# A ring of four slots for gathered table rows, and a residual that stays in SBUF

## What is computed

```python
def _peer(hn, w_query, sub_keys, expert_down, expert_up):
    q = (hn @ w_query).reshape(b, s, PEER_HEADS, 2, PEER_QUERY_DIM // 2)
    sc = jnp.einsum('bshcd,hckd->bshck', q, sub_keys)
    v1, i1 = lax.top_k(sc[..., 0, :], PEER_TOPK)
    v2, i2 = lax.top_k(sc[..., 1, :], PEER_TOPK)
    ...
    top, pos = lax.top_k(cand, PEER_TOPK)      # 8 heads x 16 experts per token
    gate = jax.nn.softmax(top, axis=-1)
    ...
        u = expert_down[ib]                    # rows of a table of 16384 x 1024
        act = jax.nn.gelu(jnp.einsum('bld,blhkd->blhk', hb, u), approximate=False)
        coef = (gb * act)
        vv = expert_up[ib]
        return jnp.einsum('blhk,blhkd->bld', coef, vv)
    ...
h = h + _peer(hn, ...)
```

## Time and profile before

| | us |
|---|---|
| median of 3 runs | 4510.15 (4506.05 to 4513.31) |
| the profiled execution | 4505.03 |
| its span, first to last instruction | 4503.1 |
| expert stage in it | from 3314.7, its first load, to the end |
| busy: TensorE, VectorE, ACT, POOL | 4046.4, 3025.7, 2273.3, 1124.3 |
| moved by DMA | 1082.32 MB, mean 240 GB/s |

### The profile page before, as it was taken

How to read it: one execution, slowest core, us unless ns; L and a number is a source line. 1 busy time by engine, 2 the same in 40 slices (tenths; PEclk the granted TensorE clock), 3 DMA queues, 4 the chain that set the end, 5 groups by cost and what they waited for, 6 DMA issues and landing times. The chain is left out here.

```text
span 4503.1 us, 60284 instructions
## 1 busy us (share of the span) xinstructions
PE 4046.4 (90%) x22760; PEld 3234.1 (72%) x22760; DVE 3025.7 (67%) x3742; ACT 2273.3 (50%) x2916; POOL 1124.3 (25%) x547
## 2 busy tenths in 40 slices
PE   6897669999999999999699779789879999999999
PEld 6786646656555655655479777678779999988887
DVE  5254468888888888888446352254489877688884
ACT  3332146667677677676325235332225998533332
POOL 2121100000000000000132222132224555666662
PEclk9898879999999999999799889899889999999999
DMA  2222079999999999999423422232236899999995
GB/s 87 66 67 78 20 269 349 359 364 368 364 368 361 360 360 367 363 369 361 149 95 94 143 73 69 84 112 71 89 117 230 302 349 348 360 361 367 368 343 191
DMA packets 506172, 1082.32 MB, mean 240 GB/s; under 512 B 23570, under 2 KB 209170, under 8 KB 494712
## 3 DMA queue, kind: packets, MB, share of 16 engines
q1 hardware_dynamic: 465416, 936.49, 58.2%
q0 software_dynamic: 40560, 143.16, 8.6%
HBM read 1001.57 MB, written 77.97 MB: 240 GB/s over the span
## 5 line engine op out<-in xcount | busy, mean ns | idle before, releaser
L1605 DVE TENSOR_TENSOR ffn_low<-ffn_raw,ffn_high 128x2048 fp32r<-128x2048 f32 (+1 forms) x576 | 1189.5, 2109 | 257.4 <-ACT ffn_high L1558 257.4
L1558 ACT CAST ffn_high<-ffn_raw 128x2048 fp32r<-128x2048 f32 (+1 forms) x576 | 987.0, 1765 | 409.2 <-DMA ffn_raw<-in_w_down 126.5
L2850 ACT CAST peer_high<-peer_raw 128x1024 fp32r<-128x1024 f32 x256 | 256.2, 1050 | 446.2 <-PE peer_ps L2832 268.1
L1452 POOL DMA_INDIRECT scratch_h<-ffn_result,ffn_y_rows x16 | 46.3, 2896 | 1344.0 <-DVE ffn_result L1597 1344.0
L296 PE MATMUL peer_ps<-peerbuf_hnT_high,peer_high 128*128 128x384 f32 x1024 | 353.2, 345 | 27.3 <-DVE peer_low L2656 23.6
L298 PE MATMUL peer_ps<-peerbuf_hnT_low,peer_high 128*128 128x384 f32 x1024 | 344.3, 336 | 0.0
L297 PE MATMUL peer_ps<-peerbuf_hnT_high,peer_low 128*128 128x384 f32 x1024 | 344.3, 336 | 0.0
L2656 DVE TENSOR_TENSOR peer_low<-peer_raw,peer_high 128x1024 fp32r<-128x1024 f32 x192 | 260.4, 1383 | 104.4 <-ACT peer_high L2850 100.8
L296 PE MATMUL ffn_gate_p<-ffn_high,ffn_x_high 128*66 128x512 f32 (+1 forms) x768 | 290.1, 378 | 21.1 <-DVE ffn_low L1605 21.1
L296 PE MATMUL ffn_up_p<-ffn_high,ffn_x_high 128*66 128x512 f32 (+1 forms) x768 | 288.2, 375 | 3.1 <-DVE ffn_low L1605 3.1
L296 PE MATMUL ffn_down_p<-ffn_high,ffn_t_high 128*66 128x512 f32 x704 | 279.9, 398 | 11.8 <-DVE ffn_low L1605 11.8
(11 more groups left out here) (522 smaller groups left out, 10004.3 us busy)
## 6 DMA issues: line engine op xcount, KB each, us to landing
ffn_raw<-in_w_gate SPq DMA_DIRECT2D x80, 2048.0 KB, 9.6
ffn_raw<-in_w_up SPq DMA_DIRECT2D x80, 2048.0 KB, 9.9
ffn_raw<-in_w_down SPq DMA_DIRECT2D x80, 2048.0 KB, 10.5
peer_raw<-in_peer_down_t SPq DMA_DIRECT2D x64, 1024.0 KB
peer_raw<-in_peer_up_t SPq DMA_DIRECT2D x64, 1024.0 KB
scratch_a<-peer_gelu SPq DMA_DIRECT2D x64, 384.0 KB
scratch_g<-peer_spread SPq DMA_DIRECT2D x24, 1024.0 KB
peer_spread<-scratch_g SPq DMA_DIRECT2D x16, 1536.0 KB, 11.9
```

The costliest lines, as they stand in the source:

```text
L1452: pool.indirect_dma_start(h_dram, bass.IndirectOffsetOnAxis(ap=y_rows[:, 0:1], axis=0), result[:, :], None, compute_op=ALU.add).then_inc(y ...
L1558: act.copy(half_of(high, q, h), half_of(raw, q, h)).then_inc(high_done, 1)
L1605: dve.tensor_tensor(half_of(low, q, h), half_of(raw, q, h), half_of(high, q, h).bitcast(F32), ALU.subtract).then_inc(low_done, 1)
L2850: act.copy(high[:, q % 2, cols], raw[:, q % PR_RAW, cols]).then_inc(high_done, 1)
```

## The change

The ring has four slots: the three tiles of `hn` and `h[:, NT, :]`. The three residual tiles of `h` stay where they are; their store, their load, both semaphores and the scratch tensor are gone. Nothing else is edited.

```diff
-ROW_RING = 7
+ROW_RING = 4
...
-        rows = [hn[:, i, :] for i in range(DENSE)] + [h[:, NT, :]] + [h[:, i, :] for i in range(DENSE)]
+        rows = [hn[:, i, :] for i in range(DENSE)] + [h[:, NT, :]]
         assert len(rows) == ROW_RING
...
                 load_down(1)
-                sp.dma_start(h_dram.rearrange("t p d -> p t d"), h[:, 0:DENSE, :]).then_inc(h_out, 16)
                 for q in range(PEER_BLOCKS + 6):
...
                 sp.wait_ge(row_used, n_rows)
-                sp.dma_start(h[:, 0:DENSE, :], h_dram.rearrange("t p d -> p t d")).then_inc(h_back, 16)
                 sp.dma_start(out[DENSE * P:NT * P, :], h[:, DENSE, :]).then_inc(stored, 16)
...
                     if n >= ROW_RING:
                         pool.wait_ge(row_used, n - ROW_RING + 1)
-                    elif n == DENSE + 1:
-                        pool.wait_ge(h_out, 16)
...
-                dve.wait_ge(h_back, 16)
                 for t in range(DENSE):
                     dve.wait_ge(tile_summed, t + 1)
```

More of the change, by code:

```diff
@@ L2579, in finish, with peer_experts @@
         dve.sem_inc(self.finished, 1)
-def peer_experts(nc, io, hn, hnT, h, ident, found, a_dram, g_dram, h_dram, out):
+def peer_experts(nc, io, hn, hnT, h, ident, found, a_dram, g_dram, out):
     plan, at = peer_plan()
@@ L2636, in peer_experts @@
             st.sem(x) for x in ("product_done", "c_high_done", "c_low_done", "tile_summed", "added", "stored"))
-        idx_done, row_used, dots_gelu, coef_done, h_out, h_back, gated, minus_done, distance, group_taken_dve = (
-            st.sem(x) for x in ("idx_done", "row_used", "dots_gelu", "coef_done", "h_out", "h_back", "gated", "minus_done",
+        idx_done, row_used, dots_gelu, coef_done, gated, minus_done, distance, group_taken_dve = (
+            st.sem(x) for x in ("idx_done", "row_used", "dots_gelu", "coef_done", "gated", "minus_done",
                                 "distance", "group_taken_dve"))
@@ L3073, in second_block @@
     g_dram = nc.dram_tensor("scratch_g", [G_LOADS, P, G_BATCHES, G_KEYS * G_BATCH], F32).ap()
-    hd_dram = nc.dram_tensor("scratch_hd", [DENSE, P, D], F32).ap()
     acum_dram = nc.dram_tensor("scratch_acum", [SSD_HEADS, SEQ], F32).ap()
@@ L3346, in second_block @@
             query_scores(nc, io, x, hn, hnT, ident, *found)
-            peer_experts(nc, io, hn, hnT, x, ident, found, a_dram, g_dram, hd_dram, out)
+            peer_experts(nc, io, hn, hnT, x, ident, found, a_dram, g_dram, out)
 def two_blocks(nc, io, out):
```

## The result

The changed kernel takes 4715.5 us (median of four runs, 4697.6 to 4719.8), the kernel before 4511.6 beside it: a ratio of 1.0447, 95% interval 1.0433 to 1.0461. It is slower, as forecast, but by 204 us where 102.5 were forecast, and outside the range. The profiled execution took 4713.3 us, with a span of 4711.5.

The account below looks back on a forecast made before the run. TensorE was taken as the bound. Residual -1, blocks without groups +6.5, entry +12 and second half +85 summed to +102.5 us on the profiled 4505.03, forecast 4607 us, range 4535 to 4680.

Parts of the forecast that it names:

- First half, blocks with group work: Blocks at 3520 to 3878: later dots delay the next low, but some 3 us of slack remain, so 0.
- Clock: 0: New TensorE pauses bring lower clock, but slower columns eat pause, not time: 0, upper bound 27 us.
- The second half: Expert stage's second 64 blocks: 5.2 us more per three blocks over 16.3 loops, +85 us.
- the right loop: Second half: c_low, a load, product, same-block gather, accumulate, lows, c_low; 12.9 + A + G = 30.3 us per three blocks.
- A: Second half: SP's load of an a tile, taken as 7.2 us for three, 12 for the fourth: 8.4 us.
- G: Second half: POOL's same-block gather of 512 KB, taken as 9.0 us, next to the waited rows.
- The five blocks without groups: First half, blocks without group work: 9.6 us each where they take 8.3 now, +6.5 us, bounds 0 and 15.
- the entry: Entry to the second half: late first product and the same-block gather behind it delay TensorE, +12 us, bounds 4 and 22.
- The residual's gain of 1 us: Store and reload gone: gain of 1 us for a quieter queue at the stage's start, bounds 0 and 3.
- worse: Rival: TensorE joins the second half's loop through ACT's split and lower clock counts; about 4740 us, chance 0.05.
- a DMA share near 0.8: Sign of the forecast case: the second half's DMA share falls to about 0.8.
- if it grows, the slack of 3 us was wrong: Sign: the first half's stretch with group work should keep its length; growth would refute its 3 us of slack.

Follow-up runs that it names:

- experiment 2: Changed kernel with a third PSUM bank for the group results: 4627.8 us, ratio 1.0255 to the kernel before.
- experiment 4: Changed kernel with each gather issued in the block in which its slot's row is used, not the block after: 4539.7 us, ratio 1.0059.
- experiment 15: Changed kernel, two PSUM banks; gathers issued as slots free in blocks 20 to 62, ahead of the product from 63; a load before weight load: 4503.2 us, ratio 0.9979.
- experiment 8: Changed kernel with filler TensorE work (third group computed three more times) ahead of its wait in the first half: 4678.4 us, ratio 1.0369.
- experiment 9: Changed kernel with 16 filler matmuls ahead of the c_low wait in every third block from 70 to 112: 4715.9 us, ratio 1.0443.
- experiment 1: Kernel before with a ring of four, its store and reload of the residual kept: 4693.6 us, ratio 1.0402.
- experiment 3: Changed kernel with POOL's gathers of a block issued ahead of its product, not behind it: 4626.9 us, ratio 1.0237.
- experiment 11: Changed kernel with SP issuing the a tile's load ahead of the block's weight and g loads: 4675.1 us, ratio 1.0358.
- experiment 10: Changed kernel with gathers of half a row, 256 KB for 512, in the second half alone: 4670.0 us, ratio 1.0352.
- experiment 12: Changed kernel with a third PSUM bank, POOL's gathers ahead of its product and SP's a load ahead of its weight load: 4515.1 us, ratio 1.0014.

## Why the prediction was right and wrong

**The failed step** is "First half, blocks with group work": "Some 3 us of slack, so 0." It took as deadline the next use of low, ACT's split at 3720.40. The deadline that comes first is another: behind the waiting dots stands, right behind the low, VectorE's copy of a group out of PSUM, and TensorE waits for it inside the same block (50.5 us over 15 in the trace after). The prediction listed what is queued behind the wait, "the weight split (low) and c_low of the next block", and left the copy out, though VectorE's order in a block has it between them and the dots. In the trace of before that copy never held anything, and no row of a wait named it. It measured +94.1 us: experiment 2 removed the wait and 90 us of it, experiments 4 and 15 the late gathers and as much.

**Its second error** is in the same step: POOL's issue times were carried over from before (3703.96, 3705.22), as if POOL ran free. POOL's gathers stand behind its half of the split, which waits for ACT's, and that waited 124.4 us for TensorE in 16 of these blocks, so a late third group delays the next gathers. That made a loop, and not a one-time shift.

**Clock: 0** failed for the first half, where TensorE is a link of the loop: 43 us (experiment 8). The Trainium skill (TensorE: Matmul & The Clock Gate, section Terms) puts the penalty of throttled time at about that time multiplied by 1 - K/N, where K of every N clock pulses pass; at 4/8 that is a half. By that rule the 95.6 us would cost 47.8, an estimate, and the 43 of experiment 8 agree. For the second half the reason given, "TensorE is not a link of the loop", does not hold as it stands: the chain passes through TensorE in five places, with 11.6 us more than at full clock. That is well under the 37 us, an estimate, that the same rule gives for the 75 us, so by the chain most of the time at the lower clock ate pause there, as the prediction said. Experiment 9 can't show it, since its added work may cancel the gain.

**The second half** came out as forecast, 91.4 us for 85, by the right loop but with two wrong sizes that cancel. These are the links of the changed kernel, the mean of the 16 turns from block 65 to 113, measured between the starts and ends of the instructions:

| link, us | taken | measured |
|---|---|---|
| c_low's end to the a load's issue | 0.1 | 0.15 |
| the a load, issue to its product's start | 8.4 | 10.1 |
| product and gap | 2.25 | 2.1 |
| gather, issue to its accumulate | 9.0 | 7.2 |
| accumulate, two lows, c_low | 4.65 | 5.0 |
| to the c_low of the next block | 5.9 | 6.6 |
| sum | 30.3 | 31.1 |

(Over all of blocks 64 to 115 it is 516.8 / 17 = 30.4.) A was 1.7 us too short. A term is missing from it: in these turns of experiments 1 and 8 the product started 1.4 and 1.8 us after the load had landed, because POOL was still issuing the gathers of the block before. G was 1.8 us too long. It had been read from the few gathers of the kernel before that VectorE waited for, 9.55 to 12.6 us, and where seven slots make most gathers early, those are the longest. In experiments 1, 8 and 9, whose second half is edited little or not at all, the same-block gathers took 5.2 to 5.3 us at the median and 5.9 to 6.1 on the mean. With only A put right the forecast of this half would have been 113 us, with only G 56; that 85 met 91 is luck in part. That the a load and the product ahead of the gather are links is shown by experiments 3 (both taken out of the gather's path) and 11 (A). Experiment 10 shortened A and G together.

By the Trainium skill's fit of 2.0 us plus bytes over 436 GB/s (DMA: Bandwidth & Descriptors, section Anatomy of one DMA, SWDGE path) a gather would take 3.2 us, an estimate, and the loop would be free. The measured gathers do not agree: the fastest of the same-block ones in these three kernels took 4.2 us from the start of their instruction, half of them over 5.2.

**The rest.** The five blocks without groups cost 4.3 us for 6.5, the entry 13.6 for 12. The residual's gain of 1 us was not seen by itself: no pair of runs differs by it alone except experiment 1 and the changed kernel, where the clock hides it. Of the rivals, *worse* had the joining of TensorE to the loop through ACT's split; the second half shows it in five places and cheaply, and the first half, where the rival did not look, in each pair of blocks. Among the signs, the waits for gathers of over 100 us, the pauses behind c_low and a DMA share near 0.8 came; and "if it grows, the slack of 3 us was wrong" was the one that spoke.

## What to carry to other kernels

A ring's depth sets how far ahead of its use a transfer is issued, and that lead, not the number of transfers in flight, was nearly all its worth here: four slots with gathers issued sooner came within 8 us of seven. Before a wait is put at nothing, list everything that stands behind it on its engine, find the earliest engine that waits for any of it, and ask whether the transfer's own issue hangs on that engine: then it is a loop, and pauses and lower clock are paid in every turn. A transfer's time read only where somebody waited for it is that of the longest transfers. A short load behind a long one in a queue can be a link too; turning the two was worth 0.3% by itself.

## What the runs showed that was not expected

The clock's fall behind a pause is not a fixed price. Pauses alike in number and sum (17, 51.5 and 54.6 us) came with 41.0 us at the lower clock in one kernel and 95.6 in another, which is 24 us of the kernel's time, and the lowest execution of experiment 11's kernel is 46 us under their median, with only 20.5 us at the lower clock there; of the others no trace was read.

In the second half a gather was quicker where the loop stalled more. The medians from issue to landing for 512 KB were 5.7 to 7.3 us in experiments 1, 2, 8 and 9 (blocks 64 to 115 in 521 to 524 us) and 8.5 us in experiment 12 (418.7 us). Half the bytes (experiment 10) took the same-block gathers from 5.2 or 5.3 us to no less than 4.2 at the median, so beside this traffic a large part of a gather's time does not go with its bytes.
